# A one-core hybrid decoder layer: x loaded and scaled first, chunk turns moved behind the next chunk, rounds released by the masking, tile 0 scored first

## The reference, cut to what matters

```
h  = rms_norm(x, norm1_w);  z = h @ w_in                 # 2048 -> 13312 columns
y_conv = (zb * conv3(zc * zx)) @ w_conv_out
y_diff = subln(diff_attn(q, k, v)) @ w_diff_out          # 8 heads; samples read 16 pages of 128 tokens each
y_mem  = mem_attn(qm, mk, mv) @ w_cross_out              # 4 heads into 256 memory tokens
x = x + (g0*y_conv + g1*y_diff + g2*y_mem) @ w_o         # g = sigmoid(zg)
h = rms_norm(x, norm2_w);  q = h @ w_peer_q              # 8 heads x 2 halves x 128
s1, s2 = q halves @ sub_keys;  top 16 of each, top 16 of the 256 sums -> expert numbers, gates
x = x + sum over 128 picks of gate * gelu(u[pick] . h) * v[pick]
```

## Time and profile before

| | us |
|---|---|
| median of 3 runs | 2830.64 (2829.07 to 2833.45) |
| profiled execution, its own time | 2829.35 |
| its span in the trace | 2827.70 |
| TensorE busy | 2469.4 (87%) |
| VectorE busy | 1412.7 (50%) |
| GpSimd busy | 1043.9 (37%) |
| ScalarE busy | 353.0 (12%) |
| HBM read | 905.80 MB, 323 GB/s over the span |

### The profile page before, as it was taken

How to read it: one execution, slowest core, us unless ns; L and a number is a source line. 1 busy time by engine, 2 the same in 40 slices (tenths; PEclk the granted TensorE clock), 3 DMA queues, 4 the chain that set the end, 5 groups by cost and what they waited for, 6 DMA issues and landing times.

```text
span 2827.7 us, 28082 instructions
## 1 busy us (share of the span) xinstructions
PE 2469.4 (87%) x9129; PEld 1588.6 (56%) x9129; DVE 1412.7 (50%) x2187; ACT 353.0 (12%) x759; POOL 1043.9 (37%) x952
## 2 busy tenths in 40 slices
PE   7999999999999999999998777777999497777777
PEld 5788888878766678888776323322333143233333
DVE  2365566973322223000167687786554656555543
ACT  2111000003221210000211111110111011111010
POOL 1065566120122210000026655656535454555542
PEclk9999999999999999999999899999899899999999
DMA  4398999695699975443379999999999989999998
GB/s 147 130 335 315 319 352 345 199 327 196 245 345 333 330 257 181 134 147 120 119 280 351 419 415 422 417 413 411 422 421 413 417 362 421 421 421 417 414 421 371
DMA packets 305394, 913.68 MB, mean 323 GB/s; under 512 B 15634, under 2 KB 195946, under 8 KB 236652
## 3 DMA queue, kind: packets, MB, share of 16 engines
q0 software_dynamic: 122304, 723.48, 63.8%
q1 hardware_dynamic: 182980, 188.92, 20.4%
HBM read 905.80 MB, written 6.56 MB: 323 GB/s over the span
## 4 chain that ended last, share of the span: by engine, by line
PE 54%; DMA 23%; DVE 12%; issue 4%; POOL 4%; ACT 2%; DVEq 0%; POOLq 0%; ACTq 0%; SPq 0%
PE ps L578 21%; PE ps L656 11%; DMA sb_S<-in_peer_u_dram,sb_ring 9%; PE ps L884 7%; DMA sb_bregion<-in_peer_u_dram,sb_ring 6%; PE ps L668 5%; DMA sb_mkv<-in_peer_u_dram,sb_ring 3%; PE ps L646 3%; PE ps L758 2%; DVE sb_bregion L1770 2%; DMA sb_S<-in_peer_v_dram,sb_ring 1%; DVE sb_S L1770 1%; DMA sb_wring<-in_peer_v_dram,sb_ring 1%; POOL sb_bregion L487 1%; DMA sb_wring<-in_w_in_dram 1%
## 5 line engine op out<-in xcount | busy, mean ns | idle before, releaser
L884 PE MATMUL ps<-sb_wring,sb_ring 128*128 128x512 f32 x992 | 464.0, 619 | 127.1 <-DMA sb_wring<-in_peer_v_dram,sb_ring 75.9
L578 PE MATMUL ps<-sb_hT,sb_wring 128*128 128x264 f32 x2304 | 530.7, 392 | 14.8 <-DMA sb_wring<-in_w_peer_q_dram 7.7
L578 PEld LDWEIGHTS ps<-sb_hT,sb_wring 128*128 128x128 f32 x2304 | 440.8, 193 | 96.9 <-issue 20.2
L884 PEld LDWEIGHTS ps<-sb_wring,sb_ring 128*128 128x128 f32 x992 | 189.6, 197 | 401.3 <-issue 265.9
L1770 DVE CUSTOM_DVE_ANT_0 sb_bregion<-sb_bregion,sb_rows 128x2048 f32<-128x2048 f32 x128 | 293.7, 2295 | 230.3 <-DMA sb_bregion<-in_peer_u_dram,sb_ring 223.2
L656 PE MATMUL ps<-sb_hT,sb_wring 128*128 128x264 f32 x1536 | 366.4, 389 | 1.9 <-DVEq L1185 1.6
L656 PEld LDWEIGHTS ps<-sb_hT,sb_wring 128*128 128x128 f32 x1536 | 287.7, 190 | 65.4 <-issue 16.4
L487 POOL DMA_INDIRECT sb_bregion<-in_peer_u_dram,sb_ring x132 | 190.0, 1440 | 280.0 <-DVEq L1185 225.5
L884 PE MATMUL ps<-sb_hT,sb_ring 128*128 128x512 f32 x496 | 231.3, 615 | 48.2 <-DMA sb_hT<-in_peer_v_dram,sb_ring 37.2
L884 PE MATMUL ps<-sb_oreg,sb_ring 128*128 128x512 f32 x496 | 227.7, 606 | 39.9 <-DMA sb_oreg<-in_peer_v_dram,sb_ring 36.1
L1152 ACT ACTIVATE sb_ring<-sb_ident,sb_ring 128x128 f32<-128x128 f32 x248 | 99.6, 402 | 912.3 <-PE ps L884 709.0
(11 more groups left out here) (350 smaller groups left out, 2539.9 us busy)
## 6 DMA issues: line engine op xcount, KB each, us to landing
sb_wring<-in_w_in_dram SPq DMA_DIRECT2D x52, 2048.0 KB
sb_ring<-in_cache_k_dram POOLq DMA_DIRECT2D x64, 512.0 KB, 6.2
sb_mkv<-in_cache_k_dram POOLq DMA_DIRECT2D x64, 512.0 KB, 6.5
sb_mkv<-in_cache_v_dram POOLq DMA_DIRECT2D x48, 512.0 KB, 7.0
sb_rows<-in_cache_v_dram POOLq DMA_DIRECT2D x47, 512.0 KB, 6.7
sb_wring<-in_w_mem_kv_dram SPq DMA_DIRECT2D x8, 2048.0 KB
sb_wring<-in_w_o_dram SPq DMA_DIRECT2D x8, 2048.0 KB
sb_wring<-in_w_peer_q_dram SPq DMA_DIRECT2D x8, 2048.0 KB
```

What stands on the lines that cost most here:

```text
L578: last = mm(ps[:, (2 * r + c) % 4, 0:NT], wring[:, r, k, c * P:(c + 1) * P], rhs[:, k, :], start=(k == 0), stop=(k == KC - 1))
L884: last = mm(ps[:, 4 * t + q, :], diag[:, k % 4, :], e_slots[v % ER][:, q * 512:(q + 1) * 512], start=False, stop=q_stop, skip_group_check= ...
```

## The change

- **Start.** x is loaded first, tile by tile, each with its own semaphore; GpSimd makes ident and ones first and issues its loads when both prompt tiles are in. TensorE runs 13 matmuls of 512 columns on constants (warm). The prompt's rows are scaled in place (tile 0 by VectorE, tile 1 by ScalarE) and transposed; only the 8 sample rows still meet a diagonal. Two one-element activations stand ahead of the loads of the tables. The state's transposes move behind x.
- **Turns.** linear() has its first four chunks outside of the loop, and the turn of a fourth chunk follows the next iteration's first chunk; the last turn of the k, v, mq chunks follows the first convolution chunk (last_rows).
- **Samples.** The conv state rows and own_maxima are done ahead of the last pair of sample tokens; the places of six small matmuls among the gates move.
- **Rounds.** sums_masked is signalled after the masking; a new semaphore sums_added, after the sum, releases columns().
- **Output projection.** Unrolled; x is transposed two chunks behind, and VectorE squares each block of 128 columns as it is added. Sub keys come first. Clearing of constants moves ahead of it.
- **Query projection.** Its first two chunks are done for tile 0 alone (PQ_PARTS), scored, then for the rest; scoring of part i-1 follows part i. Peer_v waits for all 18 parts.

```
+        PQ_PARTS = [(0, 0, P), (1, 0, P), (0, P, NT), (1, P, NT)] + [(j, 0, NT) for j in range(2, KC)]
...
+            sp.dma_start(x_rows[:, 0, :], A["x_prompt"][0, 0:P, :]).then_inc(s["x_in"], 16)
+            sp.dma_start(x_rows[:, 1, :], A["x_prompt"][0, P:2 * P, :]).then_inc(s["x_in1"], 16)
+            sp.dma_start(x_rows[0:TS, 2, :], A["x_sample"].rearrange("b t d -> (b t) d")).then_inc(s["x_in2"], 16)
             sp.dma_start(colrows[0:16, :], A["norm1_w"][0].rearrange("(k p) -> k p", p=P)).then_inc(s["cols_in"], 16)
             sp.dma_start(colrows[16:32, :], A["mem_norm_w"][0].rearrange("(k p) -> k p", p=P)).then_inc(s["cols_in"], 16)
             sp.dma_start(colrows[32:56, :], A["conv_w"][0].rearrange("w (k p) -> (w k) p", p=P)).then_inc(s["cols_in"], 16)
             sp.dma_start(colrows[56:72, :], A["norm2_w"][0].rearrange("(k p) -> k p", p=P)).then_inc(s["cols_in"], 16)
-            sp.dma_start(x_rows[:, 0:2, :], A["x_prompt"][0].rearrange("(t p) d -> p t d", p=P)).then_inc(s["x_in"], 16)
-            sp.dma_start(x_rows[0:TS, 2, :], A["x_sample"].rearrange("b t d -> (b t) d")).then_inc(s["x_in"], 16)
...
+            stream(8, w_pq, 0, C_PQ + 2, ("chunk_full", C_PQ))
...
+            st(nc.gpsimd.memset(ident[:, :], 0.0))
+            st(nc.gpsimd.affine_select(out=ident[:, :], in_=ident[:, :], compare_op=ALU.not_equal, fill=1.0, base=0,
+                                       pattern=[[-1, P]], channel_multiplier=1))
+            st(nc.gpsimd.memset(ones[:, :], 1.0))
+            pool.sem_inc(s["consts"], 1)
+
+            pool.wait_ge(s["x_in"], 16)
+            pool.wait_ge(s["x_in1"], 16)
...
+            def warm(n):
+
+                for _ in range(n):
+                    mm(ps[:, 5, :], ident[:, :], ones[:, :].unsqueeze(1).broadcast_to([P, 4, P]), start=True, stop=True)
+
             pe.wait_ge(s["consts"], 1)
+            warm(9)
             pe.wait_ge(s["cols_in"], 64)
-            nc.tensor.transpose(ps[:, 0, 0:72], colrows, ident[0:72, 0:72]).then_inc(s["cols_full"], 1)
-            pe.wait_ge(s["st_in"], 16)
-            for j in range(BC):
-                last = nc.tensor.transpose(ps[:, 1, j * 16:(j + 1) * 16], ring4[0:16, 0, j * P:(j + 1) * P], ident[0:16, 0:16])
-            last.then_inc(s["st_full"], 1)
+            nc.tensor.transpose(ps[:, 7, 0:72], colrows, ident[0:72, 0:72]).then_inc(s["cols_full"], 1)
+            warm(4)
...
-            pe.wait_ge(s["x_scaled"], 1)
+            pe.wait_ge(s["x_scaled"], 2)
             for k in range(KC):
-                if k < 2:
+                if k == 7:
                     pe.wait_ge(s["cols_ready"], 1)
                 if k >= 8:
                     pe.wait_ge(s[("xT_taken", "xT_taken2")[k % 2]], (k - 8) // 2 + 1)
-                for t, (first, n) in enumerate(TILES):
-                    last = mm(ps[:, k % 8, first:first + n], x_rows[0:n, t, k * P:(k + 1) * P], small[0:n, t, 0:n], start=True, stop=True)
-                last.then_inc(s["xT_full"], 1)
+                transpose_rows(x_rows, k, k % 8, TILES[0:2])
+                mm(ps[:, k % 8, TP:NT], x_rows[0:TS, 2, k * P:(k + 1) * P], small[0:TS, 2, 0:TS], start=True, stop=True).then_inc(s["xT_full"], 1)
             pe.wait_ge(s["xT_taken"], BC)
             pe.wait_ge(s["xT_taken2"], BC)
+            pe.wait_ge(s["st_in"], 16)
+            for j in range(BC):
+                last = nc.tensor.transpose(ps[:, 6, j * 16:(j + 1) * 16], ring4[0:16, 0, j * P:(j + 1) * P], ident[0:16, 0:16])
+            last.then_inc(s["st_full"], 1)
...
+
+                def four(i, pair, n0, first):
                     for r in range(NR):
-                        pe.wait_ge(w_landed[r], i * 16 + 16 * (g0 // NR + 1))
+                        pe.wait_ge(w_landed[r], i * 16 + 16 * pair)
                         for c in range(2):
                             q = 2 * r + c
-                            chunk(r, c, i * (2 * NR) + (c0 + q), rhs)
-                            if turn and q:
-                                turn(q - 1, i * (2 * NR) + (q - 1))
-                    if turn:
-                        turn(2 * NR - 1, i * (2 * NR) + (2 * NR - 1))
+                            chunk(r, c, i * (2 * NR) + (n0 + q), rhs)
+                            if first and q == 0:
+                                if pending:
+                                    pending()
+                            elif turn:
+                                turn((q - 1) % 4, i * (2 * NR) + (n0 - c0 + q - 1))
+
+                four(0, g0 // NR + 1, c0, True)
+                with pe.Fori(0, n_blocks // NR - 1) as i:
+                    four(i, g0 // NR + 2, c0 + 2 * NR, False)
+
+                def last_turn():
+                    turn(2 * NR - 1, 2 * n_blocks - 1)
+                return last_turn
...
+            linear(G_QKV, 4, C_QKV, hT, turner(C_QKV, R_QKV))()
...
-            linear(G_QKV + 4, 12, C_QKV + 8, hT, turner(C_QKV + 8, R_QKV + 8))
-            linear(G_CONV, 12, C_CONV, hT)
+            last_rows = linear(G_QKV + 4, 12, C_QKV + 8, hT, turner(C_QKV + 8, R_QKV + 8))
+            linear(G_CONV, 12, C_CONV, hT, pending=last_rows)
...
+                pe.wait_ge(s["sums_added"], m + 1)
...
-                if (q, k) == (2, 7):
+                if (q, k) == (2, 11):
                     spread_maxima(0, nk)
-                if (q, k) == (3, 4):
+                if (q, k) == (3, 8):
                     sum_partitions(0, nk)
...
-            linear(G_O, 8, C_O, merged, turner(C_O, R_O))
-            pe.wait_ge(s["x1_rows"], 1)
-            for k in range(KC):
-                if k >= 4:
-                    pe.wait_ge(s["h2T_taken"], k - 3)
-                transpose_rows(x_rows, k, 4 + k % 4, TILES).then_inc(s["h2T_full"], 1)
-            pe.wait_ge(s["h2T_taken"], KC)
-
...
+            o_turn = turner(C_O, R_O)
+            for j in range(KC + 2):
+                if j < KC:
+                    if j % 2 == 0:
+                        pe.wait_ge(w_landed[j // 2 % NR], 16 * (G_O // NR + j // 4 + 1))
+                    chunk(j // 2 % NR, j % 2, C_O + j, merged)
+                if 1 <= j <= KC:
+                    o_turn((j - 1) % 4, j - 1)
+                if j >= 2:
+                    k = j - 2
+                    if k == 0:
+                        pe.wait_ge(s["sk_ready"], 1)
+                    pe.wait_ge(s["rows_taken"], R_O + 2 + k + 1)
+                    if k >= 2:
+                        pe.wait_ge(s["h2T_taken"], k - 1)
+                    transpose_rows(x_rows, k, 6 + k % 2, TILES).then_inc(s["h2T_full"], 1)
+            pe.wait_ge(s["h2T_taken"], KC)
...
-                    last = mm(ps[0:n, 4 + q % 2, t * P:(t + 1) * P], zst[:, q % 2, first:first + n], skT[:, q % 2, :], start=True, stop=True)
+                    if lo <= first < hi:
+                        last = mm(ps[0:n, 4 + i % 2, t * P:(t + 1) * P], zst[:, i % 2, first:first + n], skT[:, j % 2, :], start=True, stop=True)
                 last.then_inc(s["tr_full"], 1)
 
-            linear(G_PQ, 8, C_PQ, hT, score)
-            pe.wait_ge(s["rows_taken"], 64 + 2)
-            pe.wait_ge(s["chunk_taken"], 104 + 4)
+            for i, (j, lo, hi) in enumerate(PQ_PARTS):
+                r, c = j // 2 % NR, j % 2
+                if i == 0 or j >= 2 and c == 0:
+                    pe.wait_ge(w_landed[r], 16 * (G_PQ // NR + j // 4 + 1))
+                pe.wait_ge(s["chunk_taken"], C_PQ + i + 1)
+                for k in range(KC):
+                    last = mm(ps[:, i % 4, lo:hi], wring[:, r, k, c * P:(c + 1) * P], hT[:, k, lo:hi], start=(k == 0), stop=(k == KC - 1))
+                last.then_inc(s["chunk_full"], 1)
+                if i == 1:
+                    score(0)
+                    score(1)
+                if i >= 3:
+                    score(i - 1)
+            score(len(PQ_PARTS) - 1)
+            pe.wait_ge(s["rows_taken"], R_PQ + 2 + len(PQ_PARTS))
+            pe.wait_ge(s["chunk_taken"], C_PQ + 4 + len(PQ_PARTS))
...
-            act.wait_ge(s["x_in"], 32)
+            st(A_(stat[:, 60:61], stat[:, 60:61], ACT.Square))
+            act.wait_ge(s["x_in"], 16)
             square_sums([(0, x_rows[:, 0, :], P)])
             act.sem_inc(s["x_ss"], 1)
+            st(A_(stat[:, 61:62], stat[:, 61:62], ACT.Sqrt))
             root(1, stat[:, 0:3])
+            act.wait_ge(s["x_ss2"], 1)
+            st(A_(x_rows[:, 1, :], x_rows[:, 1, :], ACT.Copy, scale=stat[:, 1:2]))
+            act.sem_inc(s["x_scaled"], 1)
...
-            to_stage(16, C_O, R_O)
-            for k in range(KC):
+            for j in range(KC + 2):
+                if j < KC:
+                    act.wait_ge(s["chunk_full"], C_O + j + 1)
+                    act.wait_ge(s["rows_taken"], R_O + j + 1)
+                    st(A_(zst[:, j % 2, :], ps[:, j % 4, 0:NT], ACT.Copy))
+                    act.sem_inc(s["chunk_taken"], 1)
...
-            act.wait_ge(s["x1_rows"], 1)
```

(51 more changed lines are left out.)

98 lines of the change are left out of this document (43 added, 55 removed).

## The result

The changed kernel takes 2804.81 us (median of 4 runs, 2800.1 to 2807.56) against 2831.18 (4 runs, 2829.07 to 2833.45) beside it: ratio 0.9904, 95% interval 0.9891 to 0.9917. It is faster, by about half of the 52.8 us forecast, and outside the range. Its profiled execution took 2807.56 (span 2805.5), 21.8 less than the one of before. That is the slowest of its four executions, so what is read from the two traces explains 21.8 us, and not the 26.4 between the medians.

The account below looks back on a forecast made before the run. The end was taken as set by the first expert gather plus the remaining bytes' DMA time. Gains summed to 61.8 us, less 9 given back, 52.8 off the profiled 2829.35: 2776.6, stated as 2777, range 2763 to 2794.

Parts of the forecast that it names:

- start: Kernel start: x loaded first and faster transposes bring the first weight chunk from 49.06 to 28.5, a gain of 20.6 us.
- q turn: Query chunks before the samples: one end-of-body turn moves, 0.9 us gained on the path to q_ready.
- root wait: VectorE's chain before the sample tokens: its 3.17 us wait for ScalarE's root shrinks to about 0.4, 2.8 gained.
- samples: After the last sample token: TensorE needs only the first sigmoid, resuming after 0.6 us in place of 3.5, 2.9 gained.
- rounds: Gate rounds: all of TensorE's 8 waits for the masking's signal go, 9.6 us gained.
- output projection: From first output chunk to first query chunk: 128.2 us in place of 135.6, 7.4 gained.
- first route: Query projection start: the route starts 9.3 us after it in place of 26.9, 17.6 gained.
- given back: From first gather to first peer_v row: peer_v waits 114 us, 7 later than before; 9 us charged, between 0 and 20.
- rival that named starving weights: Query projection: earlier gathers leave too little DMA rate for weights, 12 us more, 2789; chance 0.14.
- transposes stay slow: Kernel start: x transposes take 17.9 us in place of 9.8, or x is late; first chunk at 36, 2785; chance 0.12.
- slower: Output projection: transposes between chunks let TensorE's clock fall, 7.1 us more per chunk at half clock, up to 2890; chance 0.03.
- key pages: VectorE's chain before the samples: page traffic sets its pace, half of the 20.6 us is lost, 2787; chance 0.06.

Follow-up runs that it names:

- old places, twelfth run: Changed kernel with the five small matmuls among the gates at their old places; 2801.15 us, ratio 0.9888 to the kernel before.
- second run: Changed kernel, but GpSimd issues five of the peer_u gathers only once the 4th to 8th w_peer_q blocks have landed; 2796.55 us, ratio 0.9871.
- whole chunks: Changed kernel with the query projection in 16 whole chunks of 264 columns, no tile 0 parts first; 2811.27 us, ratio 0.9928.
- tenth run: Changed kernel with eight constant matmuls in place of four ahead of the x transposes, nothing added between them; 2802.28 us, ratio 0.9890.
- fill: Changed kernel with one more constant matmul of 128 columns ahead of each of the 16 pairs of x transposes; 2793.89 us, ratio 0.9872.
- maxima back: Changed kernel with the copy of the convolution rows and own_maxima back behind the last sample token; 2807.62 us, ratio 0.9909.
- no warm: Changed kernel without any constant matmuls ahead of x; 2806.63 us, ratio 0.9911.
- seventh run: Changed kernel with sums_masked signalled only behind the sum over heads, as before; 2815.51 us, ratio 0.9934.

## Why the prediction was wrong

By its own steps, gain forecast and gain in the two profiled executions:

| step | forecast | measured | from |
|---|---|---|---|
| start | 20.6 | 13.8 | 49.06, 35.24 |
| q turn | 0.9 | -0.2 | L1450 553.14, 566.80 before: 13.7 in all |
| root wait | 2.8 | 1.3 | 629.40, 614.46: 14.9 |
| samples | 2.9 | 3.0 | 632.93, 615.04: 17.9 |
| rounds | 9.6 | 7.4 | 1267.13, 1241.87: 25.3 |
| output projection | 7.4 | 5.6 | 1402.76, 1371.88: 30.9 |
| first route | 17.6 | 16.8 | 1440.68, 1392.99: 47.7 |
| given back | -9 | -26.3 | 1547.73, 1526.37: 21.4 |
| behind it | 0 | 0.8 | 2827.7, 2805.5: 22.2 |

**Given back** is the step that failed, 17.3 of the 30.6 us that lack. Its mechanism, GpSimd at the last query part and weights that share the DMA with gathers, was written down; its size was not worked through. Behind the first gather peer_v was to wait "106.7 plus the same 7.3 = 114"; it was 133.4. Three parts of that: the waits were 19.3, not 7.3; the chunks behind them ran at the lower clock (9.08 and 10.15 for 7.39, 4.5 us); the first four parts took 17.6 us, not 14.4 (1.4 of it in the first two, which took 8.80 us with the clock at 0.65 from 1372 to 1376, and 7.41 in old places with the clock at 1.00). The rival that named starving weights gave it 0.14 and 12 us; it was the case, and its size was short too: with it the forecast was 2789. The second run shows the cause: 2.7 us of waits, and the last chunk 22.6 earlier (1.6 of it from the start). The two late blocks took 21 us (fetched when the chunk that starts at 1397.31 was done, used at 1425.86) and 32 us (the chunk that starts at 1435.62; 1475.00) with three gathers issued meanwhile behind five others in the first case, and ten in the second, against a median of 8.2 us for w_o, which has the DMA to itself.

The deeper fault is in the first sentence of the argument, that "the end of the kernel is set by the moment of the first expert gather". The table's last column shows that, at a given V_LEAD, it is set by the first peer_v row, that is, in the changed kernel, by TensorE's last query chunk. By that rule an earlier route within the projection brings nothing by itself, since it leaves the projection's end where it is; what of the 17.6 us arrives depends on how the weights fare beside the gathers. In whole chunks the route was 8.2 later and the projection's end 8.7 later all the same, and why the weights waited more there stays open. I had priced the gap (7 later) but kept the route as the largest gain.

Why the weights are so slow beside the gathers is not shown. The DMA view of 1443 to 1475, where the second late block was under way, has these rows:

```profile
q0 software_dynamic: 1373, 9.94, 76.1%
q1 hardware_dynamic: 2802, 2.85, 26.2%
...
sb_wring<-in_w_peer_q_dram SPq DMA_DIRECT2D x2, 2048.0 KB, 29.1
```

The gathers' queue (q0) moved 7.2 KB a packet, the weights' queue (q1) 1.0 KB. The Trainium skill (DMA: Bandwidth & Descriptors, Queues, rings and completion order) says that a DMA engine takes turns between queues by the packet. The trace agrees in that the small packets got the small share of the bytes, but not one for one: two packets of weights passed for each of the gathers. No run changed a packet's size, so this stays an explanation that fits in part.

**Start**, 6.8 of them: the rival "transposes stay slow" (0.12) was the case, and its price was near (8.1 for all sixteen k; twelve were slow, and the first chunk came 6.7 late; in the other kernels with this start 4.3 to 6.5). The step that failed is "the 13 constant matmuls keep TensorE busy right up to x, so I take 9.8". They left a gap of 1.37 us, and without any gap (tenth run) the clock fell all the same, only later. The step took the clock for a matter of what comes before, when the rows show that it also depends on what runs. The fill, which holds it, brings the first chunk to 33.4; with x on time and every k at 0.68 it would be 29 by an estimate (17.1, fifteen times 0.68 to the last k, and the 1.95 from there to the first chunk in the fill run), near the 28.5, but no run held the clock at 0.68 a k.

No row shows the 0.9 us for completion in the bound of 8.6; the trace has x's second tile issued at 1.40 and used at 9.59.

**Root and q turn**, 2.6: VectorE's gain ahead of the sample tokens goes into their keys' loads. The wait for the root came back in whole chunks, maxima back and no warm (3.18, 2.75, 2.89 for 0.38), and from L1450 to the first sigmoid it took 61.94, 62.13 and 61.77 us there, 0.5 to 0.8 more than the changed kernel's 61.32. The loads' waits were taken as slack for the moved work, which was right, and not as a brake on what comes earlier, which was not.

**Rounds**, 2.2: the waits of 9.6 are gone to the full and are worth 10.3 (seventh run); the moved small matmuls, costed at nothing ("trade slots among the same chunks"), cost some 2.1 (twelfth run). **Output projection**, 1.8: a transpose of x costs 0.57 (0.37, and 7.32 for 7.12 in the chunk behind), not 0.33. Thirteen of them come to 2.5 us more than the forecast's fifteen, less some 0.8 by which turns and tail were shorter. The clock did not fall among the output chunks (1.00 from 1250 to 1360).

Right were: x first and its times, the absorbed k, v and mq turns with TensorE's wait moving to the samples (9.50), the moved maxima, the masking's release, the first route. The rivals slower, no effect and key pages played no part.

## What to carry over

- When a stage is said to start at its first transfer, look for the last gate in the issue order: here 29 gathers ran ahead and the 30th instruction waited for another engine. Compare the distance from each candidate to the end over several kernels; the one that stays constant is likely the gate.
- Transfers that begin earlier take the DMA from a prefetch of depth two. Count what is under way when each block is fetched; holding a few gathers for a block can be faster than letting all go.
- A wait of TensorE can cost more than its length: behind waits of 4.25 and 15.07 us the chunk ran 1.7 and 2.8 us longer, behind 1.69 and 0.97 us (second run) it took its usual 7.39.
